# Router logits in four column groups with the norm factor applied per token, a prefetch hint on TensorE's loop return, and two stores per expert instead of six

## The reference, cut to what matters

```
def rmsnorm(x, g):
    y = xf * lax.rsqrt(jnp.mean(xf * xf, axis=-1, keepdims=True) + EPS)
    return (y * g.astype(F32)).astype(x.dtype)

def moe(h, rw, rb, w1, w3, w2):                  # h = rmsnorm(x, norm_ffn), 264 tokens of 1024
    logits = t.astype(F32) @ rw.astype(F32) + rb.astype(F32)
    top_v, top_i = lax.top_k(logits, TOP_K)      # 2 of 8
    gates = jax.nn.softmax(top_v, axis=-1)
    ...
    for e in range(N_EXPERTS):
        out = out + combine[:, e:e + 1] * swiglu(t, w1[e], w3[e], w2[e]).astype(F32)

x = x + moe(...)
y = rmsnorm(x, p['norm_final'])
```

## Time and profile before

| | us |
|---|---|
| timed runs | 1614.21, 1618.24, 1618.81 |
| median | 1618.24 |
| profiled execution, its own time | 1627.19 |
| its span | 1625.4 |
| PE busy | 1481.6 (91%) |
| DVE busy | 477.1 (29%) |
| ACT busy | 201.2 (12%) |
| expert loop, 1106 to 1598 | 492 |
| from the last `xo1` matmul to the loop, 1065 to 1106 | 41 |
| from the last matmul to the end | 28 |

### The profile page before, as it was taken

One profiled execution on the slowest core, in us unless ns is written; L12 is line 12 of the kernel. 1 busy time (PEld: TensorE's weight loads), 2 busy tenths in 40 slices (PEclk: granted clock), 3 DMA queues, 4 the chain that ended last, 5 costly groups with the idle time before them and its releaser, 6 DMA issues.

```text
span 1625.4 us, 22293 instructions
## 1 busy us (share of the span) xinstructions
PE 1481.6 (91%) x9382; PEld 1020.6 (63%) x9382; DVE 477.1 (29%) x1304; ACT 201.2 (12%) x419; POOL 125.5 (8%) x155
## 2 busy tenths in 40 slices
PE   7998989799998999999999898868998998998993
PEld 5886666488875888878878684553443443443441
DVE  3345466441271311141169327130000000000003
ACT  2122021201121100000011211020000000000001
POOL 3003321400010200000000001010000000000001
PEclk9998787799998999999999896878999999999997
DMA  9643452374484895434444257636998998998962
GB/s 276 215 133 96 144 147 72 91 259 151 160 292 149 283 394 185 149 117 149 155 131 157 88 197 259 252 110 219 381 402 318 381 398 336 375 401 334 373 242 90
DMA packets 184778, 368.30 MB, mean 227 GB/s; under 512 B 9139, under 2 KB 117963, under 8 KB 184528
## 3 DMA queue, kind: packets, MB, share of 16 engines
q1 hardware_dynamic: 162600, 292.47, 50.6%
q0 software_dynamic: 19264, 71.22, 12.6%
q10 hardware_dynamic: 2816, 3.15, 0.6%
HBM read 339.12 MB, written 28.49 MB: 226 GB/s over the span
## 4 chain that ended last, share of the span: by engine, by line
PE 86%; DVE 6%; issue 2%; DMA 2%; POOL 1%; ACT 1%; ACTq 0%; POOLq 0%; SPq 0%; DVEq 0%
PE psum L863 31%; PE psum L1390 13%; PE psum L1275 10%; PE psum L1172 7%; PE psum L1396 6%; PE psum L1429 6%; PE psum L1435 3%; DVE ring L2083 1%; DMA ring<-in_cache_mem_v_dram 1%; PE psum L1239 1%; PE psum L1206 1%; PE psum L1017 1%; DVE ring L1873 1%; PE psum L1407 1%; PE psum L1323 0%
## 5 line engine op out<-in xcount | busy, mean ns | idle before, releaser
L863 PE MATMUL psum<-hT,ring 128*128 128x264 f32 x1168 | 274.4, 398 | 2.7 <-issue 1.6
L863 PEld LDWEIGHTS psum<-hT,ring 128*128 128x128 f32 x1168 | 227.9, 196 | 51.2 <-issue 9.4
L863 PE MATMUL psum<-arena,ring 128*128 128x264 f32 x992 | 229.5, 395 | 9.3 <-ACT arena L1634 5.0
L863 PEld LDWEIGHTS psum<-arena,ring 128*128 128x128 f32 x992 | 193.1, 195 | 44.5 <-ACT arena L1634 5.8
L1275 PE MATMUL psum<-hT,ring 128*128 128x264 f32 x704 | 157.0, 386 | 0.0
L1275 PEld LDWEIGHTS psum<-hT,ring 128*128 128x128 f32 x704 | 133.8, 190 | 22.9
L1390 PE MATMUL psum<-ring,arena 128*64 128x384 f32 (+1 forms) x704 | 137.2, 541 | 0.0
L1172 PE MATMUL psum<-ring,arena 128*128 128x256 f32 x512 | 114.0, 384 | 0.0
L1747 DVE TENSOR_TENSOR arena<-psum,rstd 128x264 f32<-128x264 f32 (+3 forms) x117 | 44.0, 394 | 233.6 <-PE psum L1275 118.8
L1172 PEld LDWEIGHTS psum<-ring,arena 128*128 128x128 f32 x512 | 98.3, 193 | 16.7 <-issue 3.0
L1390 PEld LDWEIGHTS psum<-ring,arena 128*64 128x64 f32 x704 | 49.1, 137 | 80.0 <-issue 80.0
(11 more groups left out here) (419 smaller groups left out, 1294.2 us busy)
## 6 DMA issues: line engine op xcount, KB each, us to landing
ring<-in_moe_w_dram SPq DMA_DIRECT2D x72, 1024.0 KB, 10.3
arena<-in_moe_w_dram SPq DMA_DIRECT2D x40, 1024.0 KB, 7.6
ring<-in_moe_w_dram SPq DMA_DIRECT2D x44, 768.0 KB, 9.3
ring<-in_ffn_w_dram SPq DMA_DIRECT2D x30, 1024.0 KB, 5.4
ring<-in_w_in_even_dram SPq DMA_DIRECT2D x22, 1024.0 KB, 5.4
ring<-in_cache_mem_k_dram POOLq DMA_DIRECT2D x16, 1024.0 KB, 8.0
ring<-in_cache_mem_v_dram POOLq DMA_DIRECT2D x16, 1024.0 KB, 6.7
arena<-in_moe_w_dram SPq DMA_DIRECT2D x20, 768.0 KB, 7.3
```

The costliest lines, as they stand in the source:

```text
L863: ins = mm(outs_[m][0:mw, 0:T], wv[:, k, m * mw:(m + 1) * mw], rhs(base + k), start=(base + k == 0), stop=(kc == len(chunks) - 1 and k == ...
```

## The change

1. Router. ScalarE now writes `hT = xT * gain`, without the norm factor, as each `xo1` tile is added (`gains`). The router weights are loaded into a buffer of 32 columns, zero but for 8, which GpSimd clears first. TensorE multiplies with the weights stationary: k-tiles 0 to 3 into four 32-partition groups of one bank, then 4 to 7 on top (group `logit4`). ScalarE copies the result to `lgT`; three matmuls with the matrix `sel`, a sum of four pieces of the identity, add the four groups and turn them token-major. The sum of squares is made per token (three matmuls of `rstd` against a column of ones), rooted and inverted as `frs`; the logits get factor and bias in one VectorE instruction, and the token rows get the factor as they are copied out of PSUM. The bias is now loaded for all partitions.
2. TensorE's expert loop is opened with a hint on its return.
3. The two 128 KB stores become one of 256 KB, the four 32 KB stores one of 128 KB; the semaphore counts follow.
4. One square root on ScalarE, of no use to the result, stands after the stores.

```diff
@@ groups
-    g += [("logit",)] + [("htok", c, j) for c in range(3) for j in range(2)] + [("rank",)]
+    g += [("logit4",), ("ss", FFN_NORM[1]), ("logit",)] + [("htok", c, j) for c in range(3) for j in range(2)] + [("rank",)]
@@ GpSimd
-            load(rwt[:, :, :], w["router_w"][0].rearrange("(t p) e -> p t e", p=P), "router_in")
-            load(rbt[0:1, :], w["router_b"], "router_in")
+            nc.gpsimd.memset(rwt[:, :, :], 0.0).then_inc(sem("blank_set"), 1)
+            pool.wait_ge(sem("blank_set"), 2)
+            load(rwt[:, :, 0:NE], w["router_w"][0].rearrange("(t p) e -> p t e", p=P), "router_in")
+            load(rbt, w["router_b"].to_broadcast([P, NE]), "router_in")
@@ TensorE
-            pe.wait_ge(sem("h_ready"), KT * (X_NORMS.index(FFN_NORM[1]) + 1))
+            o = begin(("logit4",))
             pe.wait_ge(sem("router_in"), 48)
-            o = begin(("logit",))
+            for i in range(2):
+                for j in range(4):
+                    k = 4 * i + j
+                    pe.wait_ge(sem("h_ready"), KT * X_NORMS.index(FFN_NORM[1]) + k + 1)
+                    ins = mm(o[32 * j:32 * j + 32, 0:T], rwt[:, k, :], hT[:, k, :], start=(i == 0), stop=(i == 1), skip_group_check=True)
+            end(("logit4",), ins)
+            o = begin(("ss", FFN_NORM[1]))
+            pe.wait_ge(sem("sq_ready"), FFN_NORM[1] + 1)
             for c in range(3):
                 n = P if c < 2 else NB
-                for k in range(KT):
-                    mm(o[0:n, c * NE:(c + 1) * NE], hT[:, k, c * P:c * P + n], rwt[:, k, :], start=(k == 0), stop=False)
-                ins = mm(o[0:n, c * NE:(c + 1) * NE], ones[0:1, 0:n], rbt[0:1, :], start=False, stop=True)
+                ins = mm(o[0:n, c:c + 1], rstd[:, c * P:c * P + n], ones[:, 0:1], start=True, stop=True, skip_group_check=True)
+            end(("ss", FFN_NORM[1]), ins)
+            o = begin(("logit",))
+            taken(pe, ("logit4",))
+            pe.wait_ge(sem("sel_ready"), 1)
+            for c in range(3):
+                n = P if c < 2 else NB
+                ins = mm(o[0:n, c * NE:(c + 1) * NE], lgT[:, c * P:c * P + n], sel, start=True, stop=True, skip_group_check=True)
             end(("logit",), ins)
...
-            with pe.Fori(0, pairs) as pair:
+            with nc.Fori(0, pairs, engines=[mybir.EngineType.PE], hint_back_edge=True) as pair:
@@ ScalarE
-            norm(7)
+            gains("xo1", "ffn", KT)
+            key = ("logit4",)
+            full(act, key)
+            free(key, af(lgT, bank(key)[:, 0:T], ACT.Copy))
+            key = ("ss", FFN_NORM[1])
+            full(act, key)
+            af(frs[:, 0:2], bank(key)[:, 0:2], ACT.Sqrt, scale=1.0 / DM, bias=eps[:, 0:1])
+            free(key, af(frs[0:NB, 2:3], bank(key)[0:NB, 2:3], ACT.Sqrt, scale=1.0 / DM, bias=eps[0:NB, 0:1]))
...
-                    for d in range(2):
-                        act.dma_start(xg_slots[0:64, bass.ds(n, 1), d * 512:(d + 1) * 512], ys[64 * d:64 * d + 64, h:h + 1, 0:512])\
-                            .then_inc(sem(f"ys_out{h}"), 16)
-                    for d in range(4):
-                        act.dma_start(xg_slots[64:CAP, bass.ds(n, 1), d * 256:(d + 1) * 256], ys[32 * d:32 * d + 32, h:h + 1, 512:768])\
-                            .then_inc(sem(f"ys_out{h}"), 16)
+                    act.dma_start(xg_slots[0:64, bass.ds(n, 1), :].rearrange("s n (d c) -> d s (n c)", d=2), ys[:, h, 0:512])\
+                        .then_inc(sem(f"ys_out{h}"), 16)
+                    act.dma_start(xg_slots[64:CAP, bass.ds(n, 1), :].rearrange("s n (d c) -> d s (n c)", d=4), ys[:, h, 512:768])\
+                        .then_inc(sem(f"ys_out{h}"), 16)
...
             act.sem_inc(sem("ys_stored"), 1)
+            af(small[:, 0:1], eps[:, 0:1], ACT.Sqrt, scale=1.0, bias=eps[:, 0:1])
@@ VectorE
-            normalized(FFN_NORM[1], "ffn", KT, xT, hT, T, sem("h_ready"))
+            ident_ = const("ident")
...
+            taken(dve, ("ss", FFN_NORM[1]))
+            v.reciprocal(frs[:, 0:2], frs[:, 0:2])
+            v.reciprocal(frs[0:NB, 2:3], frs[0:NB, 2:3]).then_inc(sem("frs_ready"), 1)
             full(dve, ("logit",))
...
-                ins = v.tensor_copy(lg[0:n, c, :], bank(("logit",))[0:n, c * NE:(c + 1) * NE])
+                ins = v.scalar_tensor_tensor(out=lg[0:n, c, :], in0=bank(("logit",))[0:n, c * NE:(c + 1) * NE], scalar=frs[0:n, c:c + 1],
+                                             in1=rbt[0:n, :], op0=ALU.mult, op1=ALU.add)
```

More of the change, by code:

```diff
@@ L173, in lin_x @@
         mem = {"wout0": [("ss", MEM_NORM[0])], "f2": [("ss", MEM_NORM[1])]}.get(name, [])
-        return [(name, 0), (name, 1)] + mem + lin(name, KT)[2:] + ([("ss", n)] if n == FFN_NORM[1] else [])
+        return [(name, 0), (name, 1)] + mem + lin(name, KT)[2:]
     def lin_ss(name, count, n):
@@ L450, in trunk_kernel @@
         back = (htok, fin)
-        rwt = R.take(KT, NE)
+        rwt = R.take(KT, 32)
         rbt = R.take(NE)
+        lgT = R.take(T)
+        sel = R.take(NE)
+        frs = R.take(3)
         lg = R.take(3, NE)
@@ L1260, in cross @@
                     taken(pe, ("ao", l, t))
-                linear(f"xo{l}", 4, [8], lambda k: oT[:, k, :], norm=FFN_NORM[1] if l else None)
+                linear(f"xo{l}", 4, [8], lambda k: oT[:, k, :])
             memory_k(0)
@@ L1645, in tokens_out @@
                         full(act, key)
-                        free(key, af(dst[0:n, c, j * 512:(j + 1) * 512], bank(key)[0:n, :], ACT.Copy))
-            tokens_out("htok", htok)
+                        free(key, af(dst[0:n, c, j * 512:(j + 1) * 512], bank(key)[0:n, :], ACT.Copy,
+                                     scale=1.0 if factor is None else factor[0:n, c:c + 1]))
+            act.wait_ge(sem("frs_ready"), 1)
+            tokens_out("htok", htok, frs)
             act.wait_ge(sem("gap_ready"), 1)
@@ L1678, in _ @@
                     act.wait_ge(sem("down_full"), n + 1)
-                    act.wait_ge(sem(f"ys_out{h}"), pair * 96 + 1)
+                    act.wait_ge(sem(f"ys_out{h}"), pair * 32 + 1)
                     af(ys[:, h, 0:512], psum[:, 6, :], ACT.Copy).then_inc(sem("ys_low"), 1)
@@ L2204, in _ @@
             cross(1)
-            normalized(FFN_NORM[1], "ffn", KT, xT, hT, T, sem("h_ready"))
+            ident_ = const("ident")
+            step(v.tensor_tensor(sel, ident_[:, 0:NE], ident_[:, 32:32 + NE], ALU.add))
+            step(v.tensor_tensor(sel, sel, ident_[:, 64:64 + NE], ALU.add))
+            v.tensor_tensor(sel, sel, ident_[:, 96:96 + NE], ALU.add).then_inc(sem("sel_ready"), 1)
             v.memset(mx[:, 2, :], 0.0)
```

8 lines of the change are left out of this document (5 added, 3 removed).

## The result

The changed kernel takes **1604.22 us** (median, 1600.68 to 1607.31, 4 runs) beside 1617.62 us (1614.21 to 1618.81, 4 runs) for the kernel before: a ratio of **0.992**, 95% interval 0.9893 to 0.9947. That is 13.4 us less, inside the range of the prediction (1591 to 1624) and 6.8 us under its point of 1611. One execution further on, of the kernel without the early table, took 2233.78 us at a granted clock of 0.64, and is left out of that kernel's median and ratio.

The account below looks back on a forecast made before the run. The prediction took TensorE work to bound the kernel almost end to end. Its terms, -3.6 - 19.5 + 10.9 + 4.9 = -7.3 us, from a 1618.24 us median gave 1611, range 1591 to 1624.

Parts of the forecast that it names:

- Router, -3.6 predicted: Router: dropping the norm work ahead of the logits and 24 narrow matmuls saves 3.6 us, bounds 2 and 5.
- The cover: Router: roots, factor, bias and top-2 search end about 1.3 us before TensorE asks for them, so they stay hidden.
- two things that end together: Before the router logits: VectorE's scaling of h and the router's loads end together near 1073; the edit removes only one.
- Back edge, -19.5 predicted: Expert loop's three returns: the hint removes idle and slow restart, 20.55 us less 1.05 left, bounds 0 and 20.5.
- Stores in the loop, +10.9 predicted: Expert loop: merged stores on 2 and 4 DMA engines delay the last weight chunk, so TensorE waits 10.9 us.
- wide stores: Rival for the expert stores: merged DMAs spread over 16 engines after all, -24.4 us, 1594; chance 0.22.
- S: Expert stores: the busiest DMA engine's work per expert, put at 7.3 us; the changes sum to zero at 8.3.
- Stores at the end, +4.9 predicted: After the last matmuls: the last expert's merged stores land later, 1607.7 in place of 1602.8, costing 4.9 us.
- Square root table, 0: Ahead of the gather: loading the table early gains 0, since VectorE's combine already covers its 1.28 us.
- main case: Expert stores: narrow stores at the loop's price, 1603 to 1620 us with S from 7.0 to 8.5; chance 0.50.
- no prefetch: Rival at the loop's return: the hint does nothing and the idle stays, +1.3 us, 1619.5; chance 0.10.
- the starved loop: Rival in the expert loop: stores on two engines starve TensorE, +19 us, 1637 at S = 10.7; chance 0.12.

Follow-up runs that it names:

- the kernel without the early table: The changed kernel without the extra square root on ScalarE behind the expert loop: 1606.1 us, 0.9905 of the kernel before.
- the router alone: The kernel before with only the router edits, keeping six stores per expert and the unhinted loop: 1616.7 us, 0.9975 of before.
- the doubled run: The changed kernel with each merged store sent twice, the second time into spare HBM rows: 1652.1 us, 1.0194 of the kernel before.
- the six-store kernel: The changed kernel with the earlier six stores per expert put back, router edits and hint kept: 1597.2 us, 0.9873 of the kernel before.
- hint alone: The kernel before with only the prefetch hint on the expert loop's return: 1602.0 us, 0.9901 of before.
- wide merged: The changed kernel with its merged stores written as 128 HBM-side pieces, rows in another order: 1597.1 us, 0.9853 of the kernel before.
- merged stores alone: The kernel before with only the two merged stores per expert: 1626.5 us, 1.0041 of before.

## Why the prediction was right, and where it was not

**Router, -3.6 predicted: right, step by step.** The trace says -4.0, the router alone -4.1 timed. The cover also held: the picks ended at 1078.2, 1.8 us before TensorE was through with the transposes; I had said 1.3. What I called one of "two things that end together", the router's loads, was worth more than the edit: 9.6 us when taken away. I had the row for it and priced only the part that the edit removes.

**Back edge, -19.5 predicted: the mechanism right, the size a little large.** Nothing is left of a return (I had left 0.35 for each), but the return itself costs less than in the earlier trace rows. In three other executions without the hint the loop is 488.9 to 489.2 us, 2.4 us shorter than in the profiled execution of before, whose first restart took 10.09 us where theirs took 8.78. That makes 17.7 to 18.1 us in traces, 16.0 timed. I worked from one execution of 1627.19 us that stood 9 us above the median, and took only the sum, not the terms, back to the median.

**Stores in the loop, +10.9 predicted: wrong, and the failed step is the base of the DMA work.** It was a sum of three: 426.6 of weights, 42.3 of narrow stores, against a need at 1574.5. The last chunk was to land at 1585.4, 479.2 us behind the loop's start; it landed at 462.7, ahead of its need at 467.6, and TensorE waited 0 us instead of 10.9. The prediction had named this as its sign of being wrong ("if the loop has no DMA wait (then 1594)"), and the sign came. It had tied the missing wait to wide stores; none of its cases with a working hint had narrow stores that cost only at the end, which is what was measured. The 426.6 came from the share of busy time, 0.97 of 1.03. The same two rows have another measure, 370 of 410 GB/s. By it the work is 453 x 370 / 410 = 408.8, the last chunk lands at 1116.5 + 408.8 + 42.3 = 1567.6, before the need, and the loop's term is 0. Counted from the loop's start and without its own stores, as in the doubled run, that base is 411, inside the 402 to 421 found there, but it was chosen after the result. With it the doubled run gives S = (504.3 - 411) / 14 = 6.7 and not 7.3, so that 1567.6 comes so near to the landing (461.4 against 462.7 behind the loop's start) is partly luck. The cause of the share's overstating the work was not tested, but that it does shows in the six-store kernel, where a stretch of the loop has a share of 1.02 with 391 GB/s:

```profile
1160.00:1440.00 280.00, 279.22 (x2759) 126.16 (x2756) 18.07 (x49) 19.92 (x39) 0.00 (x0) 1.00 1.02 391
```

Such a stream was full by its share and still had room. With six stores or wide ones the last chunk lands 26.2 us (before), 26.4 (hint alone), 27.0 (router alone), 27.8 (six stores) and 27.5 (wide merged) ahead of the loop's end, though the loops differ by 20 us. So it was TensorE leaving its slots that paced those streams, and the engines had work to spare that a share of 1.02 does not show. With merged stores and the hint 8.5 us of that lead are left, with merged stores and no hint 24.5 to 24.8.

Against the 10.9 stands the six-store run, whose loop is the changed kernel's to 0.1 us; for the mechanism stands the doubled run, +41.2. The merged stores alone decide nothing here, as said. The change went through a margin, and the doubled stores went over it. That margin is what I mis-sized. How the remainder divides between base and stores is open (above).

**Stores at the end, +4.9 predicted: right.** 5.5 in the profile, 5.0 with the merged stores alone, 6.6 timed (3.9 to 9.2). The 2 + 4 marks came as read from the 8-row store in the earlier trace rows.

**Square root table, 0: right,** with 0.4 us of cover.

**The sum.** -3.6 - 19.5 + 4.9 with the loop's term at 0 would have been -18.2, 1600.0. With the three parts as they were timed alone it is -4.1 - 16.0 + 6.6 = -13.5; measured -13.4 (-8.6 to -17.3). So my -7.3 was nearer to the result than its terms deserve: one term alone was 10.9 too high, and the point was only 6.1 off, because the hint's gain was put 3.5 too large and the end's cost 1.7 too small. That 1604 lies in the range owes something to luck as well: the range reached down to 1591 for the sake of wide stores, which did not come. By the prediction's own formula the result would need S = 6.5, below the 7.0 to 8.5 of its main case.

**The rivals.** Wide stores fell by the count of marks, no prefetch by the returns, and the starved loop did not come, though doubling shows that its point of decision exists: at twice the stores it is passed.

## What to carry to other kernels

Where a stream has to fit under a loop, do not take its work from a share of busy time: here a share of 1.02 left room, and bytes by the rate of a full stretch came nearer. Then look for the chunk whose lateness the most work follows, not for the last one. When DMAs are merged, read the leading dimension of both sides: 2 x 64 rows ran on two engines, and with the 4 x 32 rows behind them landed in 9.4 us; 128 pieces of the first store's bytes landed in 2. And where two things end together ahead of a stage, price the stage with both gone: here the loads that were left standing were worth 9.6 us, partly because a TensorE that does not idle keeps its clock.

## What the runs showed of the hardware beyond this

- An unhinted loop return of TensorE costs an idle of 3.8 to 5.1 us and then some 1.8 us more (8.78 instead of 7.02 for a group), with a granted clock of 0.60 over the first 3.8 us. With the hint the clock reads 0.99 over the whole loop and three instruction blocks fewer are fetched, 77 for 80.
- Weight chunks that landed in 16.9 us instead of 10.3 cost nothing, as long as the ring was issued far enough ahead: latency per transfer rose by two thirds, and TensorE did not see it.
- The median of the kernel before differed between groups of runs by 4 us (1617.6 to 1622.0), and identical code up to the last residual add took 1059.5 to 1065.3 us in thirteen profiles (two of them with a small load added at 550 us). A single profile can't place a few us; stretches cut at events can: the loop without its returns is within 470.3 and 471.3 in all eight kernels that weren't starved.
